# Another partition layout for the down weights of the experts, and a turn of gate and up with a column step of four

## The chip, the cores and the metric

The kernel runs on one core of one Trainium2 chip. The metric is the device time of one execution in microseconds. Everything is computed in float32, in part as pairs of rounded halves, as told below.

## The reference

Two blocks follow each other on 512 tokens of width 1024. The first has an attention part, a recurrent part and a mixture of experts; the second a convolution, a state space model and a feed-forward network. The change is in the mixture of experts. There are 32 experts in 4 groups, each token goes to the best two of its group, 16 meta tokens stand ahead but don't need an output. Cut to what matters:

```
def run_block(args):
    tok, g, e = args
    xb = x2[tok]                                            # rows of the tokens of this block
    hb = jax.nn.silu(xb @ w_gate[e]) * (xb @ w_up[e])       # [tokens, 512]
    return (hb @ w_down[e]) * g[:, None].astype(x2.dtype)   # [tokens, 1024]
```

w_gate[e] and w_up[e] are 1024 x 512 and w_down[e] is 512 x 1024, so each expert has 3 x 2 MB of weights.

## The kernel before, in words

stage_a (projections and the attention), stage_b (output projection, router, experts) and stage_c (the second block) follow each other. The change touches the experts in stage_b.

An expert takes a block of 64 token slots (SLOTS). All 32 experts run in one loop that is written out, whatever the router gave them; if an expert has more than 64 tokens, an overflow stage behind the loop, in a branch on a count, handles its further blocks (function turn of each engine, from line 1622 on).

The weights of expert e come as six units of 1 MB, each 128 partitions x 2048 values: j = 0, 1 gate, j = 2, 3 up, j = 4, 5 down. There are six buffers raw_e, one for each j. SyncE (SP) issues the loads in load (line 968) in a fixed order (gate 0, down 5 of an earlier expert, gate 1, up 2, up 3, down 4), and before each it waits until the buffer's last user, the VectorE subtraction, is done.

Each unit is split into a rounded upper part whi_e (ScalarE, line 1417) and the rest wlo_e (VectorE, line 1492), so that TensorE can run products at its fast rate and still keep the float32 accuracy. A buffer whi_e is written again only when TensorE is done with it.

TensorE goes through each expert in this order (its block in the loop over e):

- project(e, GATE, 0), lines 1567 and 1568: the 64 rows of tokens, turned and split in upper and lower halves side by side (xs, 128 columns), are the loaded operand; whi_e and wlo_e with 512 columns are the moving one. 16 matmuls. The output has 128 rows, 64 for each half of x.
- combine(e - 1), line 1581: the gate and up outputs of the expert before were copied out of PSUM by ScalarE (lines 1429 and 1436) to gate_sb and up_sb, [128 rows, 512 columns]. Each of four blocks of 128 columns is the loaded operand, st2 (two identity matrices on top of each other, 64 columns) the moving one. It adds the two halves and turns the result, so that the hidden dimension lies on the partitions: GT and UT, four blocks of 64 columns.
- x_turn(e + 1), line 1558: turns the rows of the next expert's tokens, which GpSimd gathered by an indirect transfer (line 971).
- project(e, UP, 2): another 16 matmuls.
- down(e - 2): 24 matmuls of 512 columns with hT_hi and hT_lo (the hidden values, turned and split) as loaded operand, through split_mm (lines 48 to 50).

ScalarE and VectorE make silu(GT) * UT and split it (lines 1443, 1504, 1450, 1509). The output is copied by line 1457 and scattered by GpSimd to y_rows in DRAM (line 1535).

In the gate and up weights partition p holds the eight consecutive rows 8p to 8p + 7 of the matrix. In the down weights before, partition p holds the rows p, 128 + p, 256 + p and 384 + p, and block k of the hidden values has the columns 128k to 128k + 127, which fits it. A unit of down is two such rows of 4 KB for each partition.

Of the kernel before, what the change touches and what calls it, by code (L numbers as in the profile page):

```python
# [13 lines left out]
P = 128  # L14
# [8 lines left out]
UNIT = 2048  # L23
# [3 lines left out]
N_GROUPS, PER_GROUP, N_EXPERTS, FF = 4, 8, 32, 512  # L27
SLOTS = 64
# [904 lines left out]
def stage_b(nc, dram, g, sem, banks):  # L933

    h, cols, ident, ones, eps, mixed = (g[k] for k in "h cols ident ones eps mixed".split())
# [11 lines left out]
    raw_e = [raw_all[:, j, :] for j in range(U)]  # L947
    whi_e = [hi_all[:, j, :] for j in range(U)]
    wlo_e = [lo_all[:, j, :] for j in range(U)]
    s_raw_e = [sem(f"e_raw{j}") for j in range(U)]  # L950
# [1 line left out]
                                      "ysc0 ysc1").split()}  # L952
    w_gate = dram["w_expert_gate"][0].rearrange("e (p k) f -> p e (k f)", p=P)
    w_up = dram["w_expert_up"][0].rearrange("e (p k) f -> p e (k f)", p=P)
    w_down = dram["w_expert_down"][0].rearrange("e (k p) f -> p e k f", p=P)

    def unit_source(e, j):
        if j < 4:
            w = w_gate if j < 2 else w_up
            c = UNIT * (j % 2)  # L960
            return w[:, bass.ds(e, 1), c:c + UNIT].rearrange("p o f -> p (o f)")
        k = 2 * (j - 4)
        return w_down[:, bass.ds(e, 1), k:k + 2, :].rearrange("p o k f -> p (o k) f")

    def load(sp, j, of, slot=None):
        slot = j if slot is None else slot
        place = raw_e[slot] if j < 4 else raw_e[slot].rearrange("p (k c) -> p k c", k=2)
        sp.dma_start(place, unit_source(of, j)).then_inc(s_raw_e[slot], 16)

    def gather_rows(pool, b):  # L970
        pool.indirect_dma_start(xg[0:SLOTS, :], None, m_rows, bass.IndirectOffsetOnAxis(g["row_x"][0:SLOTS, b:b + 1], 0),
# [3 lines left out]
    s = {n: sem("d_" + n) for n in (  # L975
        "gbc wr rb tr hi lo whi wlo wused out res ssq rt rs xn mtr mev log io lg mx pe gs v td "
        "cst tab pfx tabf rowx xg0").split()}
# [3 lines left out]
    with ExitStack() as tmp:  # L981
        def sb(name, shape, dt=F32):
            return tmp.enter_context(nc.sbuf_tensor(name, shape, dt))
# [26 lines left out]
        place = sb("place", [P, NT, E])  # L1010
# [342 lines left out]
    s = s_e  # L1353
# [3 lines left out]
    with ExitStack() as tmp:  # L1357
# [5 lines left out]
        st2 = sb("st2", [P, SLOTS])  # L1363
# [20 lines left out]
        def made_lo(e, j):  # L1384
            e, j = LATE.get((e, j), (e, j))
            return (s["glo"], 4 * e + j + 1) if j < 4 else (s["dlo"], 2 * e + j - 3)

        def k4(t):
            return t.rearrange("p (k c) -> p k c", k=4)

        def k2(t):
            return t.rearrange("p (k c) -> p k c", k=2)
# [155 lines left out]
        @block.tensor  # L1548
        def _(pe):
            mm = nc.tensor.matmul  # L1550

            def x_turn(e):
                pe.wait_ge(s["xg"], 16 * e + 16)
                if e >= 1:
                    pe.wait_ge(s["xlo"], e)
                for k in range(KD):
                    w = P if k == 0 else SLOTS
                    last = nc.tensor.transpose(XT[:, k * SLOTS:k * SLOTS + w], xg[0:w, k * P:k * P + P], ident[0:w, 0:w])
                last.then_inc(s["xt"], 1)

            def project(e, out, j0):
                x = xs[e % 2]
                for j in (j0, j0 + 1):
                    pe.wait_ge(*made_lo(e, j))
                    for k in range(4):
                        kk = 4 * (j % 2) + k
                        mm(out, x[:, kk, :], k4(whi[j])[:, k, :], start=kk == 0, stop=False, skip_group_check=True)  # L1567
                        last = mm(out[0:SLOTS, :], x[:, kk, 0:SLOTS], k4(wlo[j])[:, k, :], start=False, stop=kk == KD - 1,  # L1568
                                  skip_group_check=True)
                    last.then_inc(s["gused"], 1)  # L1570

            def combine(e):

                pe.wait_ge(s["gate"], e + 1)
                pe.wait_ge(s["up"], e + 1)
                if e >= 1:
                    pe.wait_ge(s["sg"], e)
                    pe.wait_ge(s["hid"], e)
                for out, t in ((GT, gate_sb[e % 2]), (UT, up_sb[e % 2])):
                    for k in range(4):  # L1580
                        last = mm(out[:, k * SLOTS:k * SLOTS + SLOTS], t[:, k * P:k * P + P], st2[:, :], start=True, stop=True)
                last.then_inc(s["comb"], 1)

            def down(e):
                pe.wait_ge(s["hlo"], e + 1)
                if e >= 1:
                    pe.wait_ge(s["y"], e)
                for j in (4, 5):
                    pe.wait_ge(*made_lo(e, j))
                    for half in range(2):  # L1590
                        for k in range(2):
                            kk = 2 * (j - 4) + k
                            c = slice(half * 512, half * 512 + 512)
                            at = LATE.get((e, j), (e, j))[1]
                            last = split_mm(nc, Y[half][0:SLOTS, :], hT_hi[e % 2][:, kk, :], hT_lo[e % 2][:, kk, :],
                                            k2(whi[at])[:, k, c], k2(wlo[at])[:, k, c], kk == 0, kk == 3)
                    last.then_inc(used(e, j)[0], 1)

            pe.wait_ge(s["st2"], 1)
            x_turn(0)  # L1600
            for e in range(E + 2):
                if e < E:
                    pe.wait_ge(s["xlo"], e + 1)
                    if e >= 1:
                        pe.wait_ge(s["gate"], e)
                    project(e, GATE, 0)
                if 1 <= e <= E:
                    combine(e - 1)
                if e + 1 < E:
                    x_turn(e + 1)  # L1610
                if e < E:
                    if e >= 1:
                        pe.wait_ge(s["up"], e)
                    project(e, UP, 2)
                if e >= 2:
                    down(e - 2)
# [5 lines left out]
    s = {n: sem("o_" + n) for n in "xg0 w xg xt xc gu sg hid ht hc down y ysc".split()}  # L1622
    g["gathers"] += [s["xg"], s["ysc"]]
    with ExitStack() as tmp:
# [4 lines left out]
        wd = sb("wd_o", [P, FF // P, D])  # L1629
        xg, xT = sb("xg_o", [P, D]), sb("xT_o", [P, KD, P])  # L1630
        row_x = g["row_x"]
        sg, hid, hidT = sb("sg_o", [P, FF]), sb("hid_o", [P, FF]), sb("hidT_o", [P, FF // P, P])
# [11 lines left out]
        def later(j):  # L1644
            return not isinstance(j, int)

        @block.sync
        def _(sp):
            def turn(j):
                if later(j):  # L1650
                    sp.wait_ge(s["down"], j)
                e = sp.value_load(over_e[0:1, bass.ds(j, 1)] if later(j) else over_e[0:1, 0:1], min_val=0, max_val=N_EXPERTS - 1)
                for w, t in ((w_gate, wg), (w_up, wu)):
                    sp.dma_start(t[:, :, :].rearrange("p k f -> p (k f)"),
                                 w[:, bass.ds(e, 1), :].rearrange("p o f -> p (o f)")).then_inc(s["w"], 16)
                sp.dma_start(wd[:, :, :], w_down[:, bass.ds(e, 1), :, :].rearrange("p o k f -> p (o k) f")).then_inc(s["w"], 16)

            blocks(sp, turn)

# [55 lines left out]
        @block.tensor  # L1715
        def _(pe):
            def turn(j):
                pe.wait_ge(s["xg"], j * 16 + 16)
                for k in range(KD):
                    last = nc.tensor.transpose(banks[2 + k // 4][:, (k % 4) * P:(k % 4 + 1) * P], xg[:, k * P:k * P + P], ident[:, :])  # L1720
                last.then_inc(s["xt"], 1)
                pe.wait_ge(s["xc"], j * 2 + 2)
                pe.wait_ge(s["w"], j * 48 + 48)
                for o, t in ((0, wg), (1, wu)):
                    for k in range(KD):
                        last = nc.tensor.matmul(banks[o], xT[:, k, :], t[:, k, :], start=k == 0, stop=k == KD - 1)
                last.then_inc(s["gu"], 1)
                pe.wait_ge(s["hid"], j + 1)
                for k in range(FF // P):
                    last = nc.tensor.transpose(banks[4][:, k * P:k * P + P], hid[:, k * P:k * P + P], ident[:, :])  # L1730
                last.then_inc(s["ht"], 1)
                pe.wait_ge(s["hc"], j + 1)
                if later(j):
                    pe.wait_ge(s["y"], j * 2)
                for half in range(2):
                    for k in range(FF // P):
                        last = nc.tensor.matmul(banks[5 + half], hidT[:, k, :], wd[:, k, 512 * half:512 * half + 512], start=k == 0,
                                                stop=k == FF // P - 1)
                last.then_inc(s["down"], 1)

            blocks(pe, turn)
# [3 lines left out]
class Weights:  # L1745
# [4 lines left out]
    SLOTS = 2  # L1750
# [1333 lines left out]
```

## Time and profile before

| | |
|---|---|
| times of 3 runs | 2245.43, 2245.93, 2250.66 us; median 2245.93 |
| the profiled execution | 2249.91 us, span 2247.7 us, mean granted TensorE clock 0.947 |
| busy, share of the span | TensorE 91%, its weight loads 73%, VectorE 61%, ScalarE 47%, GpSimd 8% |
| moved by transfers | 346.84 MB in 201776 packets, 154 GB/s over the span |
| loads of expert weights | 64 each of gate, up and down, 1024 KB each |

The page divides the span into 40 slices of some 56 us and gives the busy share of each engine in tenths. A matmul's record overlaps the next one's, so a busy TensorE in the record isn't TensorE at its peak; the distance between the starts of matmuls tells more. PE is TensorE, PEld its weight loads, DVE VectorE, ACT ScalarE, POOL GpSimd, SP SyncE. Line numbers are those of the kernel before.

### The profile page before, as it was taken

The numbers are of one execution on the slowest core, as the hardware profiler recorded it, in microseconds if no ns is written. First come the engines' busy times: TensorE is split into PE (matmuls) and PEld (weight loads), VectorE is DVE, ScalarE is ACT, GpSimd is POOL, SyncE is SP. The second block draws the span as 40 slices with busy tenths as digits, with TensorE's granted clock in tenths as the row PEclk, the third lists the DMA queues.
The fourth block names the chain that finished last, engine by engine and source line by source line (L and its number), as shares of the span: only waits on it lengthen the run. The fifth ranks groups of instructions, "written<-read, shape, count | busy, mean of one in ns | idle before, by whom it ended". The sixth has DMA issues, their size and how long they took to land. (4 is left out here: it accounts for less than half of the span.)

```text
span 2247.7 us, 25099 instructions
## 1 busy us (share of the span) xinstructions
PE 2044.9 (91%) x10173; PEld 1633.3 (73%) x10173; DVE 1361.6 (61%) x1510; ACT 1065.4 (47%) x1252; POOL 175.2 (8%) x130
## 2 busy tenths in 40 slices
PE   7999988788999999956999999988699988999997
PEld 6887677666666666635888888877478867888786
DVE  4112776588999888945298888877534453333223
ACT  4224623377888888834335444444242233322212
POOL 1000100002222222200000000000000000000000
PEclk9999899899999999985999999999899998999999
DMA  5120004289999999943333333322222213333221
GB/s 183 57 75 1 1 1 161 109 323 388 394 406 402 406 404 400 386 176 81 95 94 94 94 94 94 94 76 57 56 94 94 94 56 103 94 94 96 92 94 57
DMA packets 201776, 346.84 MB, mean 154 GB/s; under 512 B 13587, under 2 KB 149259, under 8 KB 184251
## 3 DMA queue, kind: packets, MB, share of 16 engines
q1 hardware_dynamic: 194171, 333.42, 42.4%
q0 software_dynamic: 5120, 8.40, 1.1%
q10 hardware_dynamic: 2368, 3.39, 0.5%
q8 instruction: 82, 1.34, 0.3%
q14 instruction: 35, 0.29, 0.0%
HBM read 340.91 MB, written 12.65 MB: 157 GB/s over the span
## 5 line engine op out<-in xcount | busy, mean ns | idle before, releaser
L1492 DVE TENSOR_TENSOR wlo_e<-raw_e,whi_e 128x2048 fp32r<-128x2048 f32 x190 | 431.5, 2288 | 57.5 <-ACT whi_e L1417 57.2
L1417 ACT CAST whi_e<-raw_e 128x2048 fp32r<-128x2048 f32 x188 | 359.5, 1915 | 75.2 <-PE pall L1568 46.8
L1789 DVE TENSOR_TENSOR w_lo<-w_raw,w_hi 128x2048 fp32r<-128x2048 f32 x89 | 203.8, 2290 | 288.9 <-ACT w_hi L1781 288.8
L48 PE MATMUL pall<-hT_hi,w_lo 128*128 128x512 f32 x864 | 345.6, 400 | 9.5 <-ACT xbc L2213 3.1
L1781 ACT CAST w_hi<-w_raw 128x2048 fp32r<-128x2048 f32 x89 | 169.4, 1904 | 386.7 <-PE pall L50 370.6
L49 PE MATMUL pall<-hT_lo,w_hi 128*128 128x512 f32 x864 | 340.2, 394 | 0.0
L50 PE MATMUL pall<-hT_hi,w_hi 128*128 128x512 f32 x864 | 339.5, 393 | 0.0
L1567 PE MATMUL pall<-whi_e,xs 128*128 128x512 f32 x512 | 209.7, 410 | 3.1 <-DVE xs L1497 3.1
L1568 PE MATMUL pall<-wlo_e,xs 128*64 128x512 f32 x512 | 205.8, 402 | 0.0
L48 PEld LDWEIGHTS pall<-hT_hi,w_lo 128*128 128x128 f32 x864 | 164.8, 191 | 45.9 <-issue 4.8
L50 PEld LDWEIGHTS pall<-hT_hi,w_hi 128*128 128x128 f32 x864 | 164.6, 191 | 35.0
L49 PEld LDWEIGHTS pall<-hT_lo,w_hi 128*128 128x128 f32 x864 | 164.7, 191 | 34.3 <-issue 0.5
L1567 PEld LDWEIGHTS pall<-whi_e,xs 128*128 128x128 f32 x512 | 99.2, 194 | 54.6 <-issue 4.2
L2300 DVE SCALAR_TENSOR_TENSOR mixed<-yT,cols,mixed 128x512 f32<-128x512 f32 x180 | 126.4, 749 | 0.0
L48 PE MATMUL pall<-whi_e,hT_lo 128*64 128x512 f32 x256 | 100.5, 392 | 4.1 <-issue 2.4
L48 PE MATMUL pall<-w_hi,hT_lo 128*128 128x256 f32 (+1 forms) x320 | 98.9, 309 | 5.3 <-DVE w_lo L1789 4.5
L50 PE MATMUL pall<-whi_e,hT_hi 128*64 128x512 f32 x256 | 100.6, 393 | 0.0
L49 PE MATMUL pall<-wlo_e,hT_hi 128*64 128x512 f32 x256 | 100.3, 392 | 0.0
L49 PE MATMUL pall<-w_lo,hT_hi 128*128 128x256 f32 (+1 forms) x320 | 98.0, 306 | 0.0
L50 PE MATMUL pall<-w_hi,hT_hi 128*128 128x256 f32 (+1 forms) x320 | 97.9, 306 | 0.0
L2953 DVE TENSOR_TENSOR mixed<-mixed,pall 128x512 f32<-128x512 f32 x22 | 15.1, 687 | 133.6 <-PE pall L50 133.6
L1568 PEld LDWEIGHTS pall<-wlo_e,xs 128*64 128x64 f32 x512 | 70.7, 138 | 21.6
(468 smaller groups left out, 3804.1 us busy)
## 6 DMA issues: line engine op xcount, KB each, us to landing
raw_e<-in_w_expert_up_dram SPq DMA_DIRECT2D x64, 1024.0 KB, 10.3
raw_e<-in_w_expert_down_dram SPq DMA_DIRECT2D x64, 1024.0 KB, 11.0
raw_e<-in_w_expert_gate_dram SPq DMA_DIRECT2D x64, 1024.0 KB, 10.4
w_raw<-in_w_in_dram SPq DMA_DIRECT2D x80, 512.0 KB, 6.1
w_raw<-in_w_gate_up_dram SPq DMA_DIRECT2D x44, 512.0 KB, 5.1
w_raw<-in_w_down_dram SPq DMA_DIRECT2D x22, 512.0 KB, 4.1
mixed<-in_w_in_dram SPq DMA_DIRECT2D x10, 1024.0 KB, 5.1
A<-acs_rows SPq DMA_DIRECT2D x8, 1024.0 KB, 5.0
```

Of the source, the lines that this page charges most:

```text
L48: nc.tensor.matmul(out, w_lo, m_hi, start=start, stop=False)
L49: nc.tensor.matmul(out, w_hi, m_lo, start=False, stop=False)
L50: return nc.tensor.matmul(out, w_hi, m_hi, start=False, stop=stop)
L1417: nc.scalar.copy(whi[j], raw[j]).then_inc(sem_hi, 1)
L1492: nc.vector.tensor_tensor(wlo[j], raw[j], whi[j].bitcast(F32), ALU.subtract).then_inc(sem_lo, 1)
L1567: mm(out, x[:, kk, :], k4(whi[j])[:, k, :], start=kk == 0, stop=False, skip_group_check=True)
L1568: last = mm(out[0:SLOTS, :], x[:, kk, 0:SLOTS], k4(wlo[j])[:, k, :], start=False, stop=kk == KD - 1, skip_group_check=True)
L1781: self.nc.scalar.copy(self.hi[i][:, :], self.raw[i][:, :]).then_inc(self.s_hi, 1)
L1789: (engine or self.nc.vector).tensor_tensor(self.lo[i][:, :], self.raw[i][:, :], self.hi[i][:, :].bitcast(F32), ALU.subtract).then_inc(self ...
L2300: ins = V.scalar_tensor_tensor(mixT[:, c, :], src, col("dw_w_a", k * KD + c), mixT[:, c, :], ALU.mult, ALU.add)
L2953: V.tensor_tensor(hd, sg, banks[(2 * c + 1) % 8], ALU.mult).then_inc(s["hd"], 1)
```

## The change

The down weights are laid out like gate and up: partition p gets the four consecutive rows 4p to 4p + 3, and a unit is two of them, one run of 8 KB in DRAM. So that the hidden values fit, block k of the turned gate and up output takes the columns k, k + 4, k + 8 and so on: the loaded operand of the matmuls of line 1581 is read with a column step of four. In the overflow stage the load of the down weights and the transposes of the hidden values are changed in the same way. The order of all instructions, their numbers and all waits stay.

```
-    w_down = dram["w_expert_down"][0].rearrange("e (k p) f -> p e k f", p=P)
+    w_down = dram["w_expert_down"][0].rearrange("e (p k) f -> p e (k f)", p=P)
 
     def unit_source(e, j):
         if j < 4:
             w = w_gate if j < 2 else w_up
             c = UNIT * (j % 2)
             return w[:, bass.ds(e, 1), c:c + UNIT].rearrange("p o f -> p (o f)")
-        k = 2 * (j - 4)
-        return w_down[:, bass.ds(e, 1), k:k + 2, :].rearrange("p o k f -> p (o k) f")
+        c = UNIT * (j - 4)
+        return w_down[:, bass.ds(e, 1), c:c + UNIT].rearrange("p o f -> p (o f)")
 
     def load(sp, j, of, slot=None):
         slot = j if slot is None else slot
-        place = raw_e[slot] if j < 4 else raw_e[slot].rearrange("p (k c) -> p k c", k=2)
-        sp.dma_start(place, unit_source(of, j)).then_inc(s_raw_e[slot], 16)
+        sp.dma_start(raw_e[slot], unit_source(of, j)).then_inc(s_raw_e[slot], 16)
...
                     for k in range(4):
-                        last = mm(out[:, k * SLOTS:k * SLOTS + SLOTS], t[:, k * P:k * P + P], st2[:, :], start=True, stop=True)
+                        last = mm(out[:, k * SLOTS:k * SLOTS + SLOTS], t[:, k:FF:4], st2[:, :], start=True, stop=True)
...
-                sp.dma_start(wd[:, :, :], w_down[:, bass.ds(e, 1), :, :].rearrange("p o k f -> p (o k) f")).then_inc(s["w"], 16)
+                sp.dma_start(wd[:, :, :].rearrange("p k f -> p (k f)"), w_down[:, bass.ds(e, 1), :].rearrange("p o f -> p (o f)")).then_inc(s["w"], 16)
...
-                    last = nc.tensor.transpose(banks[4][:, k * P:k * P + P], hid[:, k * P:k * P + P], ident[:, :])
+                    last = nc.tensor.transpose(banks[4][:, k * P:k * P + P], hid[:, k:FF:FF // P], ident[:, :])
```

## Rows read from the trace of the kernel before

**Rows 1.** The page: the DMA share in 40 slices, in tenths.
```profile
DMA  5120004289999999943333333322222213333221
```

**Rows 2.** Windows, 550 to 950 us: stretch, busy by engine, PEclk, DMA share, GB/s.
```profile
550.00:950.00 400.00, 390.64 (x1976) 270.06 (x1975) 360.38 (x221) 342.57 (x294) 102.86 (x48) 0.99 1.01 400
```

**Rows 3.** Line 1436, the copy of up: ns min/median/max, first and last start.
```profile
L1436 ACT COPY mixed<-pall x32: 571/581/616, 467.3 to 965.8; 128x512 f32<-128x512 f32 x32
```

**Rows 4.** Timeline of TensorE, 700 to 717 us: start us, us, what, count.
```profile
700.60 0.50 PE L1567 MATMUL pall<-whi_e,xs 128*128 128x512 f32 x1
...
713.60 1.89 PE L1581 MATMUL pall<-st,mixed 128*128 128x64 f32 x16
715.33 0.86 PE L1558 MATMUL pall<-ident,xg 128*128 128x128 f32 x8
716.12 0.51 PE L1567 MATMUL pall<-whi_e,xs 128*128 128x512 f32 x1
```

**Rows 5.** Waits, 550 to 950 us: us in total, times, longest.
```profile
ACT whi_e L1417 <- DMA raw_e<-in_w_expert_down_dram: 10.4, 12, 1.5
...
ACT whi_e L1417 <- DMA raw_e<-in_w_expert_gate_dram: 8.3, 16, 1.1
...
PE pall L1558 <- DMA xg<-m_rows,row_x: 7.7, 12, 1.4
```

**Rows 6.** Tile raw_e, 500 to 1000 us: SP's issues of loads, ns min/median/max.
```profile
L968 SPq DMA_DIRECT2D raw_e<-in_w_expert_down_dram x60: 368/379/770, 501.3 to 961.4; - x60
L968 SPq DMA_DIRECT2D raw_e<-in_w_expert_gate_dram x54: 327/328/328, 503.5 to 935.8; - x54
```

**Rows 7.** DMA queues, 465 to 500 us: packets; MB and share of 16 engines.
```profile
DMA packets 2223, 13.04 MB, mean 373 GB/s; under 512 B 328, under 2 KB 328, under 8 KB 939
...
q1 hardware_dynamic: 1980, 12.59, 93.1%
```

**Rows 8.** DMA queues, 930 to 965 us.
```profile
DMA packets 2342, 10.77 MB, mean 308 GB/s; under 512 B 303, under 2 KB 303, under 8 KB 1754
...
q1 hardware_dynamic: 2100, 10.33, 77.0%
```

**Rows 9.** DMA issues of the whole span: count, KB each, median us to landing.
```profile
raw_e<-in_w_expert_up_dram SPq DMA_DIRECT2D x64, 1024.0 KB, 10.3
raw_e<-in_w_expert_down_dram SPq DMA_DIRECT2D x64, 1024.0 KB, 11.0
raw_e<-in_w_expert_gate_dram SPq DMA_DIRECT2D x64, 1024.0 KB, 10.4
...
xg<-m_rows,row_x POOLq DMA_INDIRECT x32, 8.8
```

**Rows 10.** DMA queues and issues, 700 to 750 us.
```profile
DMA packets 3921, 20.21 MB, mean 404 GB/s; under 512 B 590, under 2 KB 590, under 8 KB 2321
...
q1 hardware_dynamic: 3440, 19.43, 97.0%
q0 software_dynamic: 480, 0.76, 4.7%
...
raw_e<-in_w_expert_gate_dram SPq DMA_DIRECT2D x7, 1024.0 KB, 11.4
raw_e<-in_w_expert_down_dram SPq DMA_DIRECT2D x6, 1024.0 KB, 11.7
```

**Rows 11.** Groups of weight loads, 550 to 950 us: busy us, mean ns, idle before.
```profile
L1568 PEld LDWEIGHTS pall<-wlo_e,xs 128*64 128x64 f32 x399 | 54.6, 137 | 16.6
L1581 PEld LDWEIGHTS pall<-st,mixed 128*128 128x128 f32 x400 | 48.5, 191 | 3.4
```

**Rows 12.** Groups of VectorE, whole span, shapes apart.
```profile
L1171 DVE SCALAR_TENSOR_TENSOR mixed<-h,rs_d,gbc_d 128x1024 f32<-128x1024 f32 x4 | 8.8, 2191 | 0.1
...
L1977 DVE SCALAR_TENSOR_TENSOR xn_j<-h,rs_j,gp 128x1024 f32<-128x1024 f32 x4 | 5.1, 1284 | 0.1
```

**Rows 13.** Groups, 960 to 1030 us: all that the overflow stage has in the trace.
```profile
L1705 DVE MEMSET xg_o<- 128x1024 f32 x1 | 0.9, 912 | 11.1 <-PEq L1357 11.1
```

## The prediction

> **What bounds the kernel now.** The time before is 2245.93 us (median of 2245.43, 2245.93 and 2250.66). The profiled execution took 2249.91 us with a span of 2247.7 us; the sum is made against it and then carried over to the median, 4.0 us lower.
>
> I first read the page's slices [rows 1]. They show where the DMA engines are full: only in the slices from about 9 to 17 of 40, some 500 to 950 us, where they move 400 GB/s [rows 2]. This is the expert loop, the one stage whose work the change touches. In the stretch from 550 to 950 us [rows 2] TensorE is busy 390.64 of 400 us, the DMA share is 1.01 and the granted clock 0.99. VectorE (360.38) and ScalarE (342.57) have some room. So two resources are full at once, TensorE and the transfers, and it must be found which of them ends last.
>
> The up output is copied once per expert, 32 times, first at 467.3 and last at 965.8 us [rows 3]: 498.5/31 = 16.08 us per expert. The timeline of TensorE for one expert [rows 4] gives what it could be: from the first gate matmul at 700.60 to that of the next expert at 716.12 is 15.52 us with no gap. In it 56 matmuls of 512 columns follow each other every 0.23 us (12.9 us), the turn of gate and up starts at 713.60 and the next work at 715.33 (1.73 us), and the turn of the gathered rows takes 0.79 us. So TensorE needs 15.5 us and an expert takes 16.1. The waits of that stretch [rows 5] show the rest: TensorE waits 12 times for the gather of rows (7.7 us), ScalarE 12 times for a down load (10.4 us) and 16 times for a gate load (8.3 us). A mean granted clock of 0.99 costs 1% of 400 us, 4 us, or 0.16 us for each of the 400/16.08 = 24.9 experts. That leaves 16.08 - 15.52 - 0.16 = 0.40 us per expert that is waiting: TensorE binds, and the transfers push it back a little.
>
> **The change part by part.**
>
> *Down loads.* 64 loads of 1 MB stay 64 loads of 1 MB. Each partition gets one run of 8 KB per load where it got two of 4 KB; gate and up loads have the 8 KB form already. On SP's queue the issue of a down load takes 379 ns and that of a gate or up load 328 ns [rows 6]. That saves 51 ns 64 times, 3.3 us, beside an SP that mostly waits for buffers to come free: nothing on the path, at most 0.05 us earlier landing each.
>
> What the form does to throughput I take from two stretches with different mixtures. From 465 to 500 us, 939 - 328 = 611 packets are between 512 B and 8 KB and 2223 - 939 = 1284 of 8 KB or more: about a fifth of the bytes came in runs of 4 KB. The queue moved 12.59 MB in 93.1% of 35 us on 16 engines, 24.1 B/ns for an engine [rows 7]. From 930 to 965 us it is 1451 against 588, over half of the bytes, and 10.33 MB in 77.0%, 24.0 B/ns [rows 8]. So a step of some 36 points in the share of 4 KB runs changes the rate by 0.8%. Down is a third of the expert bytes: at most 0.7% of the transfer time, 0.7% of 16.08 = 0.11 us per expert, 3.7 us over 32. The lower bound is zero or a little below. I take 0.05 us per expert, 1.5 us in all, since the transfers only take part in 0.40 of the 16.08 us.
>
> The other price for the same thing is the landing: 11.0 us for down against 10.3 and 10.4 for up and gate [rows 9]. But between 700 and 750 us it is 11.7 against 11.4 for gate [rows 10], and with six loads in 16.08 us some four of them are in flight at any time, so this is mostly the place in the queue. It is the upper bound and a rival below.
>
> *The matmuls of down.* The same 24 per expert, from the same slots in the same order. Row 4p+k now lies on partition p as its k-th, and the hidden values 4p+k are put into k of the turned output. Nothing is added, no wait is moved: no queue gets another order. VectorE and ScalarE read and write the same contiguous tiles. Zero.
>
> *The turn of gate and up, line 1581.* Eight matmuls per expert, each run as two loads of weights and two passes (16 of each) [rows 4]. The loaded operand is now t[:, k:512:4], one value in every 16 bytes, where it was 128 values side by side. This is the only unknown of size. The loads set the pace there: 16 of them stand for 1.73 us or 0.11 us each, while a load of 128 columns is 191 ns in the record and one of 64 is 137 [rows 11]. The 54 ns between give 0.84 ns per column, some 0.11 us for 128: the turn is nothing but loads in a row, and what one of them gains in length is on TensorE's path.
>
> No row has TensorE reading with a step. The nearest is on VectorE: a SCALAR_TENSOR_TENSOR of 1024 values with both operands at a step of 32 bytes (line 1171) takes 2191 ns, the same form without a step (line 1977) 1284 [rows 12]. That is 0.89 ns more per value. By it a load of 128 columns would be 113 ns longer, 16 of them 1.81 us per expert. Against it stands what TensorE takes in at the moving side: 512 values in 0.23 us, or four (16 bytes) in 1.80 ns, where the VectorE row with a step has 2191/1024 = 2.1 ns for each value. So the two engines' paths do not have the same limit, and the weight load asks for its values only every 0.84 ns, half as often as the moving side. The bounds are 0 and 1.81 us per expert. I take 0, as the moving rows are of the same engine, and keep the other end for the range, since they show no operand at a step.
>
> The Trainium skill speaks against the change here. "SBUF — State Buffer", section "Door 1: The DMA port swizzle", says that lines of SBUF are 16 bytes wide and that at least two accesses to a line are needed for full bandwidth; "Advanced Engine Details and Errata", section "SBUF Cachelines", has the penalty whenever each access goes to another line. The new step of 16 bytes has one access in each. VectorE's row with a step agrees with it; no row shows whether a weight load, slower per column, feels it. By the rule the time would be that of the first rival.
>
> *Overflow blocks.* Lines 1656 and 1730 lie in a branch. Of that stage the trace has the memset of line 1705 [rows 13] and no matmul of its lines, so the branch isn't entered: zero.
>
> **Sum.** 1.5 us off 2249.9 gives 2248.4 for the profiled kind of execution, 2244.4 against the median; I say 2244.5 us.
>
> **The rivals.**
>
> *The strided weight load is slow* (ends on the other side). Its place is line 1581, its price 16 x 0.113 = 1.81 us per expert. The combine stands between the gate and up products, so nothing covers it but the waiting of 0.40 us per expert, or 0.56 if the time at the lower clock level is counted too. Net (1.81 - 0.40) x 32 = 45 us to (1.81 - 0.56) x 32 = 40 us, say 42: 2288 us. It decides from 0.40/16 = 25 ns more per load on: at half the VectorE price it is (0.90 - 0.40) x 32 = 16 us, 2262. For it: [rows 12]. Against it: the moving side's rate, and the slow demand of a load.
>
> *The down loads land as the others do.* 0.7 us of 11.0 is 6%, on a third of the bytes 2.1% of 16.08, 0.34 us per expert, 11 us in all: 2235 us. For it: ScalarE waits for down loads longer than for gate loads [rows 5]. Against it: the near equal rates [rows 7, 8], and that TensorE already reaches 15.52 now and again.
>
> *Gathers come later.* The gather of the next expert's rows shares the engines with the loads, and TensorE waits for it. It takes 8.8 us [rows 9]. Where packets of the two queues take turns, each turn behind an 8 KB piece is some 0.16 us longer than behind one of 4 KB (4096 B at 25.0 B/ns, which is 19.43 MB in 97.0% of 50 us on 16 engines [rows 10]). A gather or scatter is five packets for each engine (480 for six of them on 16 engines, the same rows). For a third of five turns that is 0.27 us, at half of the experts (12 waits in 24.9): 0.27 x 16 = 4 us, 2250 us.
>
> *Nothing at all moves*: 2246 us; not told apart from the forecast.
>
> **How the numbers follow.** The forecast with "nothing moves" 0.50, the slow weight load 0.35, faster landing 0.12, later gathers 0.03. A change of 0.3% is 6.7 us, about what a measurement of this kernel can tell from none: below 2239 is faster, above 2252.7 slower. The weight load has less than 6.7 us of effect in a small part of its case (0.02), a late gather stays within it, and faster landing reaches it in most of its case (0.11, and 0.02 more from the forecast's edge): faster 0.13, same 0.52, slower 0.35. The range goes from 2237 to 2288: it leaves out half of the faster case and the quarter of the slow one that lies above 42 us. The likeliest case alone has 2241 to 2250.
>
> **What would show it.** In the profile after, the weight loads of line 1581 stay at 191 ns and the turn at 1.9 us; at 300 ns and 3.6 us the first rival holds, and the copies of up would be 17.3 us apart. The down issue on SP falls to 328 ns, and of the 2321 packets under 8 KB from 700 to 750 us [rows 10] the 6 x 256 = 1536 of the down loads are gone. The DMA share stays near 1.0 with 16.0 us per expert; if it stays full but the copies come 15.7 us apart, the transfers were the bound and the second rival is right. More waits of line 1558 for the gather speak for the third.

## The result and the profile after

| | median us | lowest to highest | runs |
|---|---|---|---|
| before | 2248.13 | 2245.43 to 2250.66 | 4 |
| changed | 2328.18 | 2320.84 to 2338.76 | 4 |

The changed kernel is slower by a ratio of 1.0361 (95% interval 1.0321 to 1.0401), some 81 us (the medians lie 80 us apart). The prediction was 2244.5 us with a range up to 2288: wrong in sign and outside its range.

The page after, DMA share in 40 slices as in [rows 1]. Behind the full slices stands a 7 where a 4 stood: the expert loop lasts longer. Behind it the span is as it was: from the start of the last copy of up [rows 3] to the end it is 2318.6 - 1036.9 = 1281.7 us, before it was 2247.7 - 965.8 = 1281.9.

```profile
span 2318.6 us, 25099 instructions
...
DMA  5210005499999999974133333314122322333221
```

The window from 550 to 950 us, for [rows 2] (PE, PEld, DVE, ACT, POOL busy, granted clock, DMA share, GB/s):

```profile
550.00:950.00 400.00, 400.00 (x1671) 288.22 (x1670) 312.23 (x189) 296.54 (x252) 57.38 (x42) 0.89 0.94 343
```

TensorE has no idle time left in the records, the transfers fell from a share of 1.01 to 0.94, and the granted clock fell from 0.99 to 0.89. The copies of up, for [rows 3], now take (1036.9 - 462.1)/31 = 18.54 us per expert, where they took 16.08:

```profile
L1435 ACT COPY mixed<-pall x32: 571/576/598, 462.1 to 1036.9; 128x512 f32<-128x512 f32 x32
```

The timeline of TensorE over one turn, for [rows 4] (the line numbers are one lower than before):

```profile
722.33 3.72 PE L1580 MATMUL pall<-st,mixed 128*128 128x64 f32 x16
725.88 0.86 PE L1557 MATMUL pall<-ident,xg 128*128 128x128 f32 x8
726.67 0.50 PE L1566 MATMUL pall<-whi_e,xs 128*128 128x512 f32 x1
727.00 0.40 PE L1567 MATMUL pall<-wlo_e,xs 128*64 128x512 f32 x1
727.25 0.56 PE L1566 MATMUL pall<-whi_e,xs 128*128 128x512 f32 x1
727.61 0.63 PE L1567 MATMUL pall<-wlo_e,xs 128*64 128x512 f32 x1
728.03 0.63 PE L1566 MATMUL pall<-whi_e,xs 128*128 128x512 f32 x1
```

Two things are to be seen here. The turn stands from 722.33 to 725.88, 3.55 us instead of 1.73. And a little behind it the matmuls of 512 columns come 0.43 us apart and no longer 0.23: the clock is at its lower level, 1.2 GHz, although TensorE works on without a pause.

The weight loads of the same stretch, for [rows 11]: 327 ns instead of 191.

```profile
L1580 PEld LDWEIGHTS pall<-st,mixed 128*128 128x128 f32 x336 | 80.0, 327 | 2.0
```

336 loads are 21 experts in 400 us, or 19.05 us each; before it were 400 loads, 25 experts, 16.0 us each.

The waits of that stretch, for [rows 5], contain no load of weights and no gather any more. ScalarE now waits for TensorE, and VectorE for ScalarE:

```profile
DVE wlo_e L1491 <- ACT whi_e L1416: 89.4, 76, 2.3
ACT whi_e L1416 <- PE pall L1567: 74.2, 47, 2.7
ACT sgT L1442 <- PE pall L1580: 24.9, 21, 1.2
```

The down loads have the new form: all are issued in 328 ns, for [rows 6], and the 2721 packets from 700 to 750 us have 585 under 8 KB, for [rows 10].

```profile
L967 SPq DMA_DIRECT2D raw_e<-in_w_expert_down_dram x53: 327/328/328, 501.6 to 996.7; - x53
```
```profile
DMA packets 2721, 18.01 MB, mean 360 GB/s; under 512 B 463, under 2 KB 463, under 8 KB 585
```

They land in 6.5 us where it took 11.0 [rows 9], and gate and up in 5.6 and 5.7. That is no gain: with 19.05 us per expert the same loads are spread over more time, and the queue in front of each is shorter.

### The profile page after: what moved, and what is told of

Read it like the earlier page. It is cut to its first block and busy times, and to the rows that moved or that the text cites. A ratio compares the mean times of both kernels' runs of the same rounds, so it can differ in the third digit from the quotient of the medians.

```text
span 2318.6 us, 25099 instructions
## 1 busy us (share of the span) xinstructions
PE 2130.9 (92%) x10173; PEld 1710.5 (74%) x10173; DVE 1366.6 (59%) x1510; ACT 1069.7 (46%) x1252; POOL 133.0 (6%) x130
## 3 DMA queue, kind: packets, MB, share of 16 engines
q10 hardware_dynamic: 2368, 3.39, 0.4%
## 5 line engine op out<-in xcount | busy, mean ns | idle before, releaser
L1566 PE MATMUL pall<-whi_e,xs 128*128 128x512 f32 x512 | 232.2, 454 | 2.2 <-DVE xs L1496 2.2
L1567 PE MATMUL pall<-wlo_e,xs 128*64 128x512 f32 x512 | 226.0, 441 | 0.0
L1566 PEld LDWEIGHTS pall<-whi_e,xs 128*128 128x128 f32 x512 | 113.2, 221 | 63.8 <-issue 22.3
L1580 PEld LDWEIGHTS pall<-st,mixed 128*128 128x128 f32 x512 | 122.0, 327 | 3.1
L1580 PE MATMUL pall<-st,mixed 128*128 128x64 f32 x512 | 119.6, 388 | 0.0
L1567 PEld LDWEIGHTS pall<-wlo_e,xs 128*64 128x64 f32 x512 | 79.2, 155 | 26.0
```

The lines of the kernel that those rows point to most:

```text
L1580: last = mm(out[:, k * SLOTS:k * SLOTS + SLOTS], t[:, k:FF:4], st2[:, :], start=True, stop=True)
```

## The experiments

All ratios are to the kernel before, run on the same chip beside each. Theory A: the step of 16 bytes in the loaded operand makes the turn slow, and the clock falls behind it. Its rival B: the 8 KB runs disturb transfers and gathers.

**The turn alone (e1).**

```
-        c = UNIT * (j - 4)
-        return w_down[:, bass.ds(e, 1), c:c + UNIT].rearrange("p o f -> p (o f)")
+        return w_down[:, bass.ds(e, 1), j - 4:4:2, :].rearrange("p o k f -> p (o k) f")
...
-                            kk = 2 * (j - 4) + k
+                            kk = (j - 4) + 2 * k
```

> The changed kernel, but with each down unit made of two rows that don't lie side by side (4p and 4p+2, 4p+1 and 4p+3), so that a partition again gets two runs of 4 KB; the gate and up output is still turned with the column step of four. Theory A (the step slows the weight loads of the turn, and the clock falls behind them): the time is that of the changed kernel, a ratio of 1.036 to the kernel before, weight loads of the turn at 327 ns, granted clock about 0.89 from 550 to 950 us. Theory B (the 8 KB runs disturb the transfers or the gathers, and with them TensorE): the time is back at the kernel before, within 0.5%. If both take part, it lies between.

Measured: 2333.66 us, ratio 1.0378 (1.0348 to 1.0408). Its window from 550 to 950 us:

```profile
550.00:950.00 400.00, 400.00 (x1670) 288.07 (x1669) 310.78 (x188) 295.03 (x250) 57.38 (x42) 0.89 0.94 342
```

The weight loads of the turn take 327 ns again. The runs of 4 KB are back and nothing of the loss is gone. B is out.

**The layout alone (e2).**

```
-                        last = mm(out[:, k * SLOTS:k * SLOTS + SLOTS], t[:, k:FF:4], st2[:, :], start=True, stop=True)
+                        last = mm(out[:, k * SLOTS:k * SLOTS + SLOTS], t[:, k * P:k * P + P], st2[:, :], start=True, stop=True)
```

> The changed kernel with the turn's operand read side by side again (128 columns in a row), so only the down loads have the new form; the hidden values are then paired with other rows of the down weights, which changes what is computed and nothing of the work. Theory A: within 0.5% of the kernel before (ratio 0.995 to 1.003), weight loads of the turn at 191 ns, about 16.0 us per expert, clock 0.99 from 550 to 950 us. Theory B: a ratio of 1.02 to 1.036.

Measured: 2242.05 us, ratio 0.9977 (0.9949 to 1.0004).

```profile
550.00:950.00 400.00, 390.82 (x1958) 269.20 (x1958) 361.65 (x224) 343.27 (x295) 105.73 (x50) 0.98 1.01 402
```

The stretch is that of [rows 2] again. The 8 KB runs are worth some 0.2%, with an interval that goes from 0.5% to nothing. The two halves of the change together give the whole loss to the turn.

**A step of two (e3, e10).** Partition p gets the rows 2p and 2p + 1 of each half of the matrix, so a load is still one run of 8 KB.

```
+    w_down = dram["w_expert_down"][0].rearrange("e (a p b) f -> p e a (b f)", a=2, p=P)
...
+                        last = mm(..., t[:, 256 * (k // 2) + k % 2:256 * (k // 2) + 256:2], st2[:, :], ...)
```

> Down weights with two consecutive rows per partition in each half of the matrix (256a + 2p + b), so that a load is one run of 8 KB for each partition, and the gate and up output is turned with a column step of two (8 bytes). Theory A1 (a 128-column load of weights takes double where each value lies in another 16 byte line, and no more where two lie in one): weight loads of the turn stay at 191 ns, the time is within 0.5% of the kernel before. Theory A2 (any step costs, or the cost grows with it): loads between 225 and 327 ns, a ratio of 1.01 to 1.036.

Measured: 2246.37 us, ratio 0.9988 (0.9972 to 1.0004).

```profile
L1579 PEld LDWEIGHTS pall<-st,mixed 128*128 128x128 f32 x388 | 49.5, 196 | 3.4
```
```profile
702.65 1.99 PE L1579 MATMUL pall<-st,mixed 128*128 128x64 f32 x16
704.47 0.88 PE L1556 MATMUL pall<-ident,xg 128*128 128x128 f32 x8
```

196 ns against 191: a step of two is as good as free. What it does cost is seen in the turn, which here stands from 702.65 to 704.47, 1.82 us and not 1.73: 0.09 us per expert or at most 3 us over 32. The times of this kernel and of the one before it here (2246.37 and 2242.05 us) don't tell that from nothing.

It was measured once more, with more runs:

> The kernel with the step of two and 8 KB runs once more, in five rounds, as it is the one that could beat both: 0.9988 of the kernel before (0.9972 to 1.0004) in three. If the longer runs of the down loads help by the 0.1 to 0.2% that the forecast gave them, 0.998 to 0.999 with an interval that ends below 1; else 1.000.

Measured: 2241.37 us, ratio 0.9977 (0.9953 to 1.0000). Two runs point the same way, by 3 to 5 us, and neither interval lies clear of 1. It is the fastest version here that computes what the kernel before computes, but it isn't shown to beat that kernel.

**The turn twice, side by side (e4).** In the kernel before:

```
-                for out, t in ((GT, gate_sb[e % 2]), (UT, up_sb[e % 2])):
+                for out, t in ((GT, gate_sb[e % 2]), (UT, up_sb[e % 2])) * 2:
```

> The kernel before with the eight matmuls of each turn issued twice, all operands side by side: TensorE gets 1.7 us more per expert, as much as the step of four adds, but with weight loads at full pace. Theory C (the fall of the clock comes with the slow loads themselves): a pace of about 17.3 us per expert with a granted clock of 0.97 or more from 550 to 950 us, 1.2 us x 31 = 38 us more than before, a ratio of 1.015 to 1.02. Theory D (any 1.7 us of short matmuls more, or a TensorE that no longer waits for transfers, brings the lower clock): clock about 0.9 and a ratio of 1.033 to 1.04 as in the changed kernel.

Measured: 2275.56 us, ratio 1.0131 (1.0100 to 1.0162). Window, and the turn in the timeline of TensorE:

```profile
550.00:950.00 400.00, 400.00 (x2219) 291.09 (x2218) 342.01 (x208) 322.57 (x277) 99.42 (x46) 1.00 1.01 379
```
```profile
707.88 3.68 PE L1581 MATMUL pall<-st,mixed 128*128 128x64 f32 x32
711.40 0.85 PE L1558 MATMUL pall<-ident,xg 128*128 128x128 f32 x8
```

The turn is as long as in the changed kernel (3.52 us against 3.55), TensorE has no idle time either, but the clock stays at 1.00. 737 loads by 32 are 23.0 experts in 400 us, 17.4 us each. The pace and the clock are those of theory C, the ratio lies a little under its 1.015 to 1.02. So a turn of that length costs 1.3% when the clock stays up (it is even a little better here than before), and the rest of the 3.6% comes with the lower clock, which a long turn of loads at full pace doesn't bring.

**The slow turn spread out (e5).** The changed kernel, each of the eight matmuls of the turn put between the two products of a row block of gate:

```
                         mm(out, x[:, kk, :], k4(whi[j])[:, k, :], start=kk == 0, stop=False, skip_group_check=True)
+                        if between:
+                            between.pop(0)()       # one matmul of the turn, t[:, k:FF:4]
                         last = mm(out[0:SLOTS, :], x[:, kk, 0:SLOTS], k4(wlo[j])[:, k, :], ...)
```

> The changed kernel (step of four), but the eight matmuls of a turn are no longer in a row: each stands between the upper and the lower product of one of the eight row blocks of gate. The first of its two slow loads then runs beside a matmul of 512 columns, the second stays bare: 8 x 0.10 = 0.8 us more per expert than with short loads, less some 0.4 us for the loads of 64 columns that follow. Theory E (the clock falls because 3.3 us in a row are nothing but slow loads): granted clock 0.97 or more from 550 to 950 us, a ratio to the kernel before of 1.00 to 1.01. Theory F (the number of slow loads per expert lowers the clock, wherever they stand): clock about 0.9, a ratio of 1.02 to 1.03.

Measured: 2284.42 us, ratio 1.0156 (1.0125 to 1.0188), so the clock is that of theory E, but the time lies between what E (up to 1.01) and F (from 1.02) gave.

In this kernel line 1584 is the turn and 1569 the lower product.

```profile
550.00:950.00 400.00, 380.87 (x1857) 278.82 (x1856) 340.43 (x211) 324.79 (x280) 104.05 (x48) 1.00 0.99 381
```
```profile
702.87 0.40 PE L1569 MATMUL pall<-wlo_e,xs 128*64 128x512 f32 x1
703.93 0.42 PE L48 MATMUL pall<-whi_e,hT_lo 128*64 128x512 f32 x1 [0.67 <-issue]
...
709.48 0.40 PE L1566 MATMUL pall<-whi_e,xs 128*128 128x512 f32 x1
709.71 0.45 PE L1584 MATMUL pall<-st,mixed 128*128 128x64 f32 x2
709.97 0.42 PE L1569 MATMUL pall<-wlo_e,xs 128*64 128x512 f32 x1
...
715.51 0.85 PE L1557 MATMUL pall<-ident,xg 128*128 128x128 f32 x8
```

With the same 16 slow loads per expert, but never more than two in a row, the clock stays up. Gate and turn together take 715.51 - 709.48 = 6.03 us, against 3.68 + 1.73 = 5.41 before. What I had not counted is a new wait: down starts 1.06 us behind the up product and not 0.23. The view of waits names no engine for it (16.8 us in the stretch, 22 times), but the timeline of ScalarE does:

```profile
702.83 1.00 ACT L1456 COPY mixed<-pall 64x1024 f32<-64x1024 f32 x1
```

Down writes the two PSUM banks out of which ScalarE copies the output of the expert before, and waits for that copy. In all 23 experts of the stretch down starts 0.1 us behind the end of this copy; in e4 it is 1.2 to 1.3 us, so the copy was no hindrance there. ScalarE works in a fixed order, and ahead of this copy stands the copy of the gate product, which now ends later since the turn is inside it (24.2 us of waiting for line 1569, 23 times). So the move made a second engine late, and that took back most of what it saved.

**A step of two, spread out (e6).** The same on the kernel with the step of two.

> The kernel with the step of two and 8 KB runs, with its turn's matmuls spread in the gate product in the same way. Eight short matmuls are each followed by a load of 64 instead of 128 columns, so 8 x 0.05 = 0.4 us less of TensorE per expert, if loads set the pace. If TensorE is the bound that ends last: 12 us less than before, a ratio of 0.995. If the transfers (share 1.0) hold the pace of 16.1 us: no difference, 0.998 to 1.0.

Measured: 2258.07 us, ratio 1.0038 (1.0009 to 1.0067), slower and not faster, which neither of its two cases gave. The gain of 0.4 us was not on a path that ended last: TensorE waits for the gathered rows 18.9 us in the stretch, where it was 7.3 in e3 and 7.7 before [rows 5], and another 5.0 us in front of down as in e5 (0.6 in e3).

```profile
PE pall L1556 <- DMA xg<-m_rows,row_x: 18.9, 19, 2.0
```

**Only gate with the step of four (e7).**

```
+                        last = mm(..., (t[:, k:FF:4] if out is GT else t[:, k * P:k * P + P]), st2[:, :], ...)
```

> The changed kernel, but only the four matmuls that turn gate have the step of four; up is turned side by side, which changes what is computed (up is paired with other columns of gate). Half the slow loads, 0.83 us more per expert, all but some 0.4 us of it on the path. If the fall of the clock needs the whole slow stretch: clock 0.97 or more from 550 to 950 us and a ratio of 1.005 to 1.01. If it is in proportion to the slow loads: clock about 0.94 and a ratio of 1.018.

Measured: 2255.89 us, ratio 1.0034 (1.0014 to 1.0053).

```profile
550.00:950.00 400.00, 400.00 (x1938) 285.44 (x1937) 357.11 (x218) 337.03 (x290) 100.14 (x48) 0.99 1.01 397
```
```profile
703.67 2.75 PE L1580 MATMUL pall<-st,mixed 128*128 128x64 f32 x16
706.25 0.86 PE L1557 MATMUL pall<-ident,xg 128*128 128x128 f32 x8
```

Half the slow loads make the turn 2.58 us long (+0.85), but cost a tenth of the whole loss, not half; against e2, which has the same down loads, it is (1.0034 - 0.9977) of 0.038, a seventh. The clock is that of the first case of the expectation (0.99), the time is a little under it. The waiting for transfers gives way first: TensorE's is gone from this stretch.

**Steps of three and of eight (e8, e9).**

```
+                        last = mm(..., t[:, k:k + 382:3], st2[:, :], ...)      # three
+                        last = mm(..., h[:, 0, k:D:8], st2[:, :], ...)         # eight
```

> The changed kernel with a column step of three (12 bytes) in the turn, which changes what is computed. If a load of weights is slow where each value lies in another 16 byte line than the one before: with 12 bytes three of four steps go to a new line and one stays, so three quarters of the extra 135 ns, about 290 ns; if two values in one line in a row are not needed and only a step of 16 bytes or more costs, 191 to 200 ns; if the cost is per step size, about 280 ns.

> The changed kernel, but the operand that the turn loads is every eighth value (32 bytes) of a row of the residual, which lies still in this stage; this changes what is computed. The turns so far stand for 0.108, 0.167 and 0.221 us per load with steps of one, three and four values: 1.30 and 1.73 ns per column with three and four, three quarters of a line of 16 bytes and a whole one. Theory L (a line of 16 bytes costs 1.73 ns, and a load takes the longer of this and its own pace): with eight, still one line per value, loads stay at 327 ns and the turn at 3.3 us, a time near the changed kernel's. Theory S (the span of bytes counts): 3.5 ns per column, loads of some 550 ns, a turn of 7 us.

Measured: 2274.94 us with three and 2340.24 us with eight, one run each. The loads of weights:

```profile
L1580 PEld LDWEIGHTS pall<-st,mixed 128*128 128x128 f32 x382 | 70.1, 261 | 2.3
```
```profile
L1580 PEld LDWEIGHTS pall<-st,h 128*128 128x128 f32 x320 | 77.7, 333 | 1.9
```

From the first matmul of a turn to the 16th the starts in the records are 1.618, 1.703, 2.502, 3.319 and some 3.39 us apart with steps of 1, 2, 3, 4 and 8. The first distance of each turn is short (some 0.06 us), since the first loads run beside the matmul ahead of the turn. The 14 others are even: 111.6, 117.7, 174.7, 233.2 and 238.0 ns on the mean. Per column of 128 that is 0.87, 0.92, 1.37, 1.82 and 1.86 ns. (The expectation above took all 15 as equal, and so has 1.30 and 1.73 for three and four.)

Theory L holds: where loads stand in a row, a line of 16 bytes costs 1.82 ns, and a column takes that times the share of a line that it needs: half a line with a step of two (0.91), three quarters with three (1.37), one with four, and not more with eight. Where the load's own 0.87 ns is longer, that counts. The three other figures come out of these two numbers within some 2%. The rule was made from steps up to four, and the step of eight tested it, in one run. The expectation of 290 ns for three was wrong since it added the two; the longer one counts. Granted clock: 0.96 with three, 0.86 with eight, though the turn with three is no longer than that of e7 (both 2.5 us): there every load is slow, in e7 half of them.

## Why the prediction was wrong

*The step that failed is the price of the strided weight load.* It had the bounds 0 and 1.81 us per expert and I took 0, "as the moving rows are of the same engine". Measured are 327 - 191 = 136 ns in the record of a load and 3.55 - 1.73 = 1.82 us in the turn: the upper bound itself. The row I leaned on, the moving side's 512 values in 0.23 us, has no operand with a step, so it could not carry the 0; no run here gives the moving side a step either. The steps of three and of eight show that the line is what costs. A load with one value per line is held to 1.82 ns per column, twice its own pace of 0.87. The 0.89 ns per value of VectorE [rows 12] was the better neighbour (1.82 - 0.87 = 0.95). That it came so near is in part luck: it is another engine at twice the step, with two operands.

*The first rival had the mechanism of the direct part, and half the price.* It gave 42 us; 81 were measured. Its direct part stood well. Of 1.8 us, some 0.40 per expert were covered by waiting: e4, whose turn is as long, shows 17.4 - 16.0 = 1.4 us per expert. Over 32 experts this would be 45 us. e4 measured 29 (0.0131 x 2248), and some 8 us of gain by its better clock hide in that (below), so 37. That is less than 45, as the experts outside the stretch lose less: over all 31 distances of the copies of up, e4 takes 16.92 - 16.08 = 0.84 us more.

*What it lacked is the clock.* In the records of the changed kernel the expert stage has some 119 us at 1.2 GHz, in 24 pieces. 23 of them begin 3 to 5 us behind the first matmul of a turn that stands for 3.55, the last 6 us. Before there were 20 us, in e4 3. At the lower level the matmuls of 512 columns come 0.427 us apart, at the upper 0.230, so a stretch there costs 46% of its length. By this estimate the clock cost (119 - 20) x 0.46 = 46 us against the kernel before, and direct 37 and clock 46 make 83, where 81 were measured. Against e4 it is (119 - 3) x 0.46 = 53 us, where (1.0361 - 1.0131) x 2248 = 52 were measured.

That the slow loads must stand in a row, and that not their number does it, was tested by e5 alone (clock 1.00 with the same loads spread out); e7, e8 and e9 fit it. How the chip comes to its choice stays open. Nothing in the prediction spoke of the clock as a follower of the change, though the row with 0.99 stood in it.

*The Trainium skill's rule* on 16-byte lines ("SBUF — State Buffer", Door 1; "Advanced Engine Details and Errata", SBUF Cachelines), which I had set beside the sum and not in it, was right on this chip in that two accesses to a line are enough and one is not: 196 ns with a step of two, 327 with four. In the same section Door 1 the Trainium skill also says that one can stride 4 fp32 values for free; here a step of four is not free for a weight load, by the same 327 ns.

*The down loads.* Forecast 0.05 us per expert, 1.5 us; e2, e3 and e10 measured 2 to 6 us less than before with intervals that reach 1. In sign and size this fits the upper bound of 3.7 us from [rows 7, 8]; it isn't shown apart from zero. The second rival (11 us, a ratio of 0.9951) lies outside the intervals of e3 and e10 and at the very edge of that of e2. The issue time, the packets and the empty overflow branch came as said.

*Later gathers* (third rival): in e2 the wait for them is 8.1 us in the stretch against 7.7, so no harm by 8 KB packets is to be seen.

*The chances.* The slow load had 0.35 for itself, with its one neighbouring row and the Trainium skill's rule beside it, and against it an argument that no row had shown. That was too little; and the range ended where the rival without its consequence did.

## What to carry to other kernels

A loaded operand of TensorE with a step is as good as free as long as two float32 values share 16 bytes (a step of two). With three, weight loads in a row take some one and a half times as long, with four or eight twice. The moving operand was not tried. Prefer a layout that needs a step of two: it kept the long DRAM runs at a cost too small to measure here.

Where a saturated TensorE gets a row of loads that run at half pace (here 3.3 us), look at the granted clock and don't count only the added time: here the clock cost more (some 46 us) than the work (some 37 us). Half of the slow work, or all of it spread between long matmuls, left the clock alone. But spreading has a price of its own: the product that it is spread in ends later, and so does what other engines do in a fixed order behind it.

## What was not expected

A line of 16 bytes costs 1.82 ns on the load side, and the moving side takes 16 bytes in 1.80 ns. They look like the same limit and aren't, as the lower clock shows. There the moving side slows down with the clock, from 0.230 to 0.427 us for 512 columns. The slow loads don't: in the changed kernel, e1 and e9 eight distances between them lie wholly in a piece at 1.2 GHz, at 233 to 240 ns, where they are 233 and 238 at 2.4 GHz.

The clock fell with TensorE busy without a pause, behind 3.3 us of slow loads (granted clock 0.89), and did not behind 3.5 us of fast ones (1.00).
